# More row tokens, packed remainders and remainders on GpSimd in a hybrid encoder block

## The reference, cut to what matters

```python
q = (xf @ w_pq).reshape(t, 8, 2, 128)
sc = jnp.einsum("thpd,hpnd->thpn", q, sub_keys)
vals, idx = lax.top_k(sc, 16)
...
best, pos = lax.top_k(cand, 16)
eidx = jnp.take_along_axis(cidx, pos, axis=-1)
g = jax.nn.softmax(best, axis=-1)
...
ue = jnp.take(u, it, axis=0)
act = gelu(jnp.einsum("td,tkd->tk", xt, ue)) * gt
ve = jnp.take(v, it, axis=0)
return jnp.einsum("tk,tkd->td", act, ve)
```

## Time and profile before

| | |
|---|---|
| runs (us) | 1620.82, 1621.73, 1619.15; median 1620.82 |
| profiled execution | span 1618.1 us; no separate time is recorded for it; the median of the runs is 2.7 us more |
| TensorE busy | 1570.4 us (97%) |
| VectorE busy | 1403.7 us (87%) |
| ScalarE, GpSimd busy | 641.8 us (40%), 624.0 us (39%) |
| DMA | 436.11 MB, mean 270 GB/s |
| granted TensorE clock | 9 tenths or more in 37 of 40 slices, 8 in three; 1.00 in the expert stage |

### The profile page before, as it was taken

One profiled execution on the slowest core, in us unless ns is written; L12 is line 12 of the kernel. 1 busy time (PEld: TensorE's weight loads), 2 busy tenths in 40 slices (PEclk: granted clock), 3 DMA queues, 4 the chain that ended last, 5 costly groups with the idle time before them and its releaser, 6 DMA issues.

```text
span 1618.1 us, 23763 instructions
## 1 busy us (share of the span) xinstructions
PE 1570.4 (97%) x7899; PEld 1291.7 (80%) x7899; DVE 1403.7 (87%) x2781; ACT 641.8 (40%) x955; POOL 624.0 (39%) x531
## 2 busy tenths in 40 slices
PE   6999999999999999999999999999999999999997
PEld 3777764665557899988888888898888888888886
DVE  6888877764999999979888998989999998989886
ACT  4234654241122666663333333333333333333233
POOL 0000000010555500016655666656555676767520
PEclk8999999989999999999999999999999999999998
DMA  8432215542212355589999999999999999999981
GB/s 349 167 150 79 79 52 197 221 155 78 92 72 73 106 205 199 209 307 402 402 380 386 375 380 389 394 392 387 355 396 358 387 362 398 347 380 355 403 301 64
DMA packets 127851, 436.11 MB, mean 270 GB/s; under 512 B 12832, under 2 KB 35360, under 8 KB 122016
## 3 DMA queue, kind: packets, MB, share of 16 engines
q1 hardware_dynamic: 74112, 247.92, 41.2%
q0 software_dynamic: 52224, 184.62, 29.6%
q10 hardware_dynamic: 1440, 2.62, 0.4%
HBM read 407.29 MB, written 27.79 MB: 269 GB/s over the span
## 4 chain that ended last, share of the span: by engine, by line
PE 71%; DVE 19%; DMA 4%; issue 3%; ACT 2%; POOL 0%; DVEq 0%; SPq 0%; ACTq 0%; POOLq 0%
PE ps L970 23%; PE ps L900 23%; PE ps L671 10%; PE ps L662 6%; PE ps L958 3%; DMA graw<-gmat 3%; PE ps L827 3%; DVE low L1886 2%; DVE Vs L1874 1%; DVE Us L1857 1%; DVE big L1886 1%; DVE att L1713 1%; DVE att L1724 1%; DVE big L1711 1%; DVE big L1729 1%
## 5 line engine op out<-in xcount | busy, mean ns | idle before, releaser
L970 PE MATMUL ps<-Vs,As 128*128 128x512 f32 x2286 | 535.6, 390 | 2.5 <-DVE As L1877 2.5
L970 PEld LDWEIGHTS ps<-Vs,As 128*128 128x128 f32 x2286 | 425.9, 188 | 86.1 <-DVE Vs L1874 1.6
L900 PE MATMUL ps<-xs,Us 128*128 128x336 f32 x2832 | 461.2, 318 | 5.1 <-DVE Us L1857 4.2
L900 PEld LDWEIGHTS ps<-xs,Us 128*128 128x128 f32 x2832 | 441.4, 188 | 22.6 <-issue 10.0
L594 POOL DMA_INDIRECT big<-pv,islot x176 | 255.9, 1454 | 144.6 <-DVE low L1916 50.9
L1338 ACT ACTIVATE big<-ps 128x352 f32<-128x352 f32 x96 | 44.7, 465 | 340.4 <-PE ps L900 281.2
L1874 DVE TENSOR_TENSOR Vs<-big,Vs 128x1024 fp32r<-128x1024 f32 x127 | 155.2, 1222 | 17.1 <-ACT Vs L1344 14.3
L662 PE MATMUL ps<-big 128*128 128x512 f32 (+1 forms) x416 | 160.3, 544 | 1.3 <-ACT big L1040 1.3
L1916 DVE SCALAR_TENSOR_TENSOR low<-big,low 128x1024 f32<-128x1024 f32 x128 | 157.0, 1280 | 0.0
L1344 ACT ACTIVATE Vs<-big 128x1024 fp32r<-128x1024 f32 x127 | 134.0, 1055 | 42.9 <-PE ps L970 40.7
L594 POOL DMA_INDIRECT low<-pu,islot x88 | 119.7, 1360 | 72.5 <-DVE colv L1886 53.9
(11 more groups left out here) (249 smaller groups left out, 2087.2 us busy)
## 6 DMA issues: line engine op xcount, KB each, us to landing
big<-puT SPq DMA_DIRECT2D x128, 512.0 KB, 3.5
big<-pv SPq DMA_DIRECT2D x64, 1024.0 KB
big<-stream SPq DMA_DIRECT2D x31, 1024.0 KB, 5.2
gmat<-big SPq DMA_DIRECT2D x11, 2048.0 KB, 7.3
graw<-gmat SPq DMA_DIRECT2D x30, 512.0 KB
low<-wada SPq DMA_DIRECT2D x28, 512.0 KB, 4.8
work<-wada SPq DMA_DIRECT2D x14, 512.0 KB, 5.6
graw<-gmat SPq DMA_DIRECT2D x15, 384.0 KB
```

The source lines that it names most:

```text
L900: mm = nc.tensor.matmul(ps[:, 6 + e, DEAD:ET], a, xs[:, b, k, :], start=(k == 0 and a is hi and b == 0), stop=(k == KT - 1 and a is lo))
L970: mm = nc.tensor.matmul(ps[:, 2 * b + half, :], a, v_parts[:, w, half * T:(half + 1) * T], start=(opens and a is hi and w == 0), stop=(las ...
```

## The change

- The row tokens grow from 176 to 192: 64 of block 1 instead of 48 (NEXT = 4, XTOK = 64). NROWS becomes 192, XB 64, ET 320; 80 turns of the gate matrix are built, in ten pieces. The dots lie in groups 2 to 61, the additions in 62 to 123.
- `As` holds, for each slot, 640 columns: 64 of remainders, the 320 rounded values, 256 of remainders. For the first token block, whose 64 dense tokens fill half of a weight tile, the tile has remainders in one half of its columns and rounded values in the other. It is multiplied by V's rounded values and by V's remainders, 2 x 2 products instead of 3 x 2, and the two halves of the sum are added at the end by a product with a folding matrix. The other two blocks are as before.
- The activations' remainders are subtracted by GpSimd (`rest_a`), in two instructions of 64 and 256 columns, between its fetches. GpSimd's program is written out in full instead of looping; the index is read from `eidx`, without the copy to `islot`.
- V comes in another order from HBM, so that two tiles are one run of 8 KB on each partition.
- The fourth set of 16 extra tokens needs a fourth spread of normalised tokens (`repeat_ext`), a fourth accumulator and 16 more small DMAs. The fold moves from group 114 to group 126, into banks 6 and 7. The order of the last blocks is 0, 2, 1, 3.

The core of the diff:

```diff
-NEXT = 3
+NEXT = 4
...
-UB = 60
-VE = 122
+UB = 62
+VE = 124
...
-DEAD = XTOK - XB
+HALF = P - XB
+ORDER = (0, 2, 1, 3)
...
-        As = sb("As", [P, 2, 2, DT], f32r)
+        As = sb("As", [P, 2, 2 * ET], f32r)
...
+        def a_hi(A):
+
+            return A[:, HALF:HALF + ET]
...
+        def dots_by(o):
+
+            return NROWS * min(max(o - 1, 0), UB - 2) // (UB - 2)
+
+        def adds_by(o):
+
+            return NROWS * min(max(o - UB + 1, 0), VE - UB) // (VE - UB)
+
+        def taken_by(o):
+
+            return dots_by(o) + adds_by(o)
...
                 sp.wait_ge(vlo_ready, g * BODY + 2 * e + 2)
-                sp.dma_start(vraw[:, e % 2, :, :],
-                             pv[bass.ds((g * BODY + 2 * e) * P, 2 * P), :].rearrange("(a p) f -> p a f", p=P)
+                sp.dma_start(vraw[:, e % 2, :, :].rearrange("p a f -> p (a f)"),
+                             pvP[bass.ds(g * (BODY // 2) + e, 1), :, :].rearrange("a p f -> (a p) f")
                              ).then_inc(v_here[e % 2], 16)
...
-            def fetch(table, places, it, r0, first=False):
-                for half in range(2):
-                    if not first or half:
-                        pool.wait_ge(row_used, it * (2 * DOTS) + (r0 + half * DOTS - ROWBUF + 1))
-                    nc.gpsimd.tensor_copy(islot[:, half, :], eidx[:, bass.ds(it * (2 * DOTS) + half * DOTS, DOTS)]
-                                          ).then_inc(slot_copied, 1)
-                    pool.wait_ge(slot_copied, it * 2 + (r0 // DOTS + half + 1))
-                    nc.gpsimd.sem_inc(pool_turn, 1)
-                    for s in range(DOTS):
-                        r = half * DOTS + s
-                        if s and not (first and r < ROWBUF):
-                            pool.wait_ge(row_used, it * (2 * DOTS) + (r0 + r - ROWBUF + 1))
-                            nc.gpsimd.sem_inc(pool_turn, 1)
-                        nc.gpsimd.indirect_dma_start(
-                            out=places[r % ROWBUF], out_offset=None, in_=table,
-                            in_offset=bass.IndirectOffsetOnAxis(ap=islot[:, half, s:s + 1], axis=0)
-                            ).then_inc(row_here[r % ROWBUF], 16)
+            def fetch(r):
+
+                if r >= ROWBUF:
+                    pool.wait_ge(row_used, r - ROWBUF + 1)
+                if r == NROWS:
+                    pool.wait_ge(alo_ready, 2 * (EVERY * (-(-4 * D // ET)) + 3))
+                table, places, c = (pu, u_row, r) if r < NROWS else (pv, v_row, r - NROWS)
+                nc.gpsimd.indirect_dma_start(
+                    out=places[c % ROWBUF], out_offset=None, in_=table,
+                    in_offset=bass.IndirectOffsetOnAxis(ap=eidx[:, c:c + 1], axis=0)
+                    ).then_inc(row_here[r % ROWBUF], 16)
+
+            def rest_a(o):
+
+                A = As[:, o % 2, :] if o < XT - 1 else Al
+                if o % EVERY == EVERY - 1:
+                    act_t = early[:, o // EVERY, :]
+                else:
+                    act_t = gel[:, (o - o // EVERY) % 2, :]
+                hi = a_hi(A).bitcast(f32)
+                pool.wait_ge(ahi_ready, o + 1)
+                nc.gpsimd.tensor_tensor(A[:, 0:HALF], act_t[:, 0:HALF], hi[:, 0:HALF], ALU.subtract).then_inc(alo_ready, 1)
+                nc.gpsimd.tensor_tensor(A[:, HALF + ET:2 * ET], act_t[:, HALF:ET], hi[:, HALF:ET], ALU.subtract).then_inc(alo_ready, 1)
...
-            fetch(pu, u_row, 0, 0, True)
-            with pool.Fori(1, NROWS // (2 * DOTS)) as it:
-                fetch(pu, u_row, it, 0)
-            pool.wait_ge(alo_ready, EVERY * (-(-4 * D // DT)) + 3)
-            with pool.Fori(0, NROWS // (2 * DOTS)) as it:
-                fetch(pv, v_row, it, NROWS)
+            for r in range(ROWBUF):
+                fetch(r)
+            r = ROWBUF
+            for o in range(XT):
+                rest_a(o)
+                while r < 2 * NROWS and r - ROWBUF < taken_by(o):
+                    fetch(r)
+                    r += 1
...
-                        mm = nc.tensor.matmul(ps[:, 6 + e, DEAD:ET], a, xs[:, b, k, :],
+                        mm = nc.tensor.matmul(ps[:, 6 + e, 0:ET], a, xs[:, b, k, :],
...
             def output_block(o, b, a_parts, v_parts, last=False, opens=False):
-                hi, lo = (a_parts[:, w, b * P:(b + 1) * P] for w in range(2))
-                for a, w in ((hi, 0), (hi, 1), (lo, 0)):
+                if b == 0:
+                    both = a_parts[:, 0:P]
+                    pairs = ((both, 0), (both, 1))
+                else:
+                    hi, lo = (a_parts[:, c + b * P:c + (b + 1) * P] for c in (0, ET - HALF))
+                    pairs = ((hi, 0), (hi, 1), (lo, 0))
+                for i, (a, w) in enumerate(pairs):
                     for half in range(2):
                         mm = nc.tensor.matmul(ps[:, 2 * b + half, :], a, v_parts[:, w, half * T:(half + 1) * T],
-                                              start=(opens and a is hi and w == 0), stop=(last and a is lo))
+                                              start=(opens and i == 0), stop=(last and i == len(pairs) - 1))
                 return mm
 
+            def fold_halves(src, part, begins=False, ends=False):
+
+                for half in range(2):
+                    mm = nc.tensor.matmul(ps[:, 6 + half, :], part, src[:, half * T:(half + 1) * T],
+                                          start=begins, stop=ends)
+                return mm
...
             def last_two():
...
                     output_block(o + 1, b, Al, Vl, True).then_inc(v_done, 1)
+                    if b == 1:
+                        pe.wait_ge(unfolded_ready, 1)
+                        fold_halves(unfolded, fold, ends=True).then_inc(folded, 1)
...
-                    if last and d == 2:
+                    if last and d == BODY - 2:
+                        pe.wait_ge(gel_ready, XT + 2)
                         pe.wait_ge(row_used, NROWS + XTOK)
                         for q in range(NEXT):
-                            for half in range(2):
-                                nc.tensor.matmul(ps[:, half, :], gath[q], acc_ext[q][:, half * T:(half + 1) * T],
-                                                 start=False, stop=False)
+                            fold_halves(acc_ext[q], gath[q], begins=(q == 0))
...
-            f(piece[:, FIRST % PRING, :, 0:DEAD], zeros[:, 0:DEAD].unsqueeze(1).broadcast_to([P, NK, DEAD]), ACT.Copy)
...
-                dve.wait_ge(ahi_ready, o + 1)
-                v.tensor_tensor(A[:, 1, XB:DT], act_t, A[:, 0, XB:DT].bitcast(f32), ALU.subtract).then_inc(alo_ready, 1)
...
+        "pvP": A(peer_v)[0].reshape(XT // 2, 2, P, D).transpose(0, 2, 1, 3).reshape(XT // 2, P, 2 * D),
```

More of the change, by code:

```diff
@@ L86, with build @@
 BANKS = 4
-def build(nc, stream, wada, skT, xT, cols, rows, biasd, identd, puT, pu, pv, gmat, hsave, out):
+def build(nc, stream, wada, skT, xT, cols, rows, biasd, identd, puT, pvP, pu, pv, gmat, hsave, out):
     f32, f32r, i32, u32 = mybir.dt.float32, mybir.dt.float32r, mybir.dt.int32, mybir.dt.uint32
@@ L358, in build, with pslot, all_stored @@
         y_sum, y_sq, y_std, y_out = sem("y_sum"), sem("y_sq"), sem("y_std"), sem("y_out")
+        def pslot(k):
+            return (k - FIRST) % PRING
         def stored(k):
-            return 16 * sum(1 for q in range(FIRST, k) if q % PRING == k % PRING)
+            return 16 * sum(1 for q in range(FIRST, k) if pslot(q) == pslot(k))
+        def all_stored(eng):
+            for k in range(PIECES, PIECES + PRING):
+                eng.wait_ge(piece_out[pslot(k)], stored(k))
         def rest_after(n):
             return (n - GAP) * BUILT // (EARLY + 1 - GAP) + 1
+        def dots_by(o):
[4 more added lines that the diff above has]
+            return dots_by(o) + adds_by(o)
         def freed(eng, n):
@@ L502, in load_turn @@
                     if first and e == 2:
-                        for k in range(PRING):
-                            sp.wait_ge(piece_out[k], stored(PIECES + k))
+                        all_stored(sp)
                     if not (first and e < 2):
@@ L1249, in _, with repeat_ext @@
                 f(n_tok[:, half * T:(half + 1) * T], ps[:, 6 + half, :], ACT.Copy).then_inc(side_free, 1)
-            for q in range(NEXT):
+            def repeat_ext(q):
                 f(nrep[q].rearrange("p k (h t) -> p k h t", h=PH),
@@ L1254, in _ @@
                   ).then_inc(spread_ready, 1)
+            for q in range(NEXT - 1):
+                repeat_ext(q)
             def gelu_early(n):
@@ L1336, in dense_turn @@
                         before = 3 if d % EVERY < 2 else 2
[L1337 removed]
+                        act.wait_ge(alo_ready, o * 2 + 2 * (1 + 3 - before))
                         f(gel[:, i % 2, :], ps[:, 6 + i % 2, 0:ET], ACT.Gelu).then_inc(gel_ready, 1)
@@ L1362, in _ @@
             dense_turn(TURNS - 1, True)
-            for b in range(TB):
-                deviation(b)
```

(31 more changed lines are left out.)

115 lines of the change are left out of this document (57 added, 58 removed).

## The result

The changed kernel takes 1683.49 us, median of 4 runs (1679.81 to 1686.2), against 1620.16 us before (4 runs beside it): ratio 1.0387, 95% interval 1.0369 to 1.0405. Its profiled span is 1677.6 us, 59.5 us more than before. The forecast was 1669 us with a range of 1604 to 1716: direction and size came out, the mechanism only in part.

The account below looks back on a forecast made before the run. TensorE bounds the kernel before; after, VectorE plus GpSimd's subtractions at 7.32 (dots) and 7.45 us a group (additions) against 6.95: +53, less 5 outside, +48 on 1620.8 gives 1669 us, range 1604 to 1716.

Parts of the forecast that it names:

- TensorE's bound lifted: Expert stage: TensorE sets the pace before; fewer output products and narrower hidden products take it from 6.84 to 6.28 us a group.
- VectorE by itself, 6.05 and 6.18: Expert stage: VectorE's own work after the change, 6.05 us a group in the dots and 6.18 in the additions.
- The port, 1.02 us added to VectorE: Expert stage: GpSimd's two subtractions and VectorE take turns, adding 1.02 us a group: 7.07 in dots, 7.20 in additions.
- The rival in which the port costs part of its length: Expert stage: a held instruction's fixed part runs meanwhile, 6.9 to 7.05 us a group, total 1610 to 1628; chance 0.11.
- Both engines near 7.2, VectorE sets the end: Expert stage: GpSimd's queue, 6.2 to 8.0 us a group, middle 7.1, is as near the bound as VectorE, 7.07 and 7.20.
- The rival with 8.0: Expert stage: GpSimd's queue is the bound at 8.0 us a group, +123 us, total 1744; chance 0.09.
- The added 0.25: Expert stage: loss of two engines taking turns at the same load, 0.25 us a group, giving 7.32 in dots, 7.45 in additions.
- The start: Before the expert stage: 80 instead of 84 turns of the gate matrix, with less work in them, save 6.5 us.
- The transfers, 6.83 and 6.70 us at 404 GB/s: Expert stage: DMA needs 6.83 us a group in dots and 6.70 in additions, hidden under 7.3 and the next limit.
- The rival of the free port: Expert stage: GpSimd and VectorE don't hold each other up, DMA is the bound, 1593 to 1605 us; chance 0.15.
- The end, +3.7: Kernel end: 8 instead of 6 folding products, +1.9 us; second output block waits for 20 products instead of 12, +1.8.
- What would show it: Expert stage signs: subtractions much over 0.29 and 0.72 us, VectorE near 99%, TensorE 90% or less awaiting As, DMA 0.92.

Follow-up runs that it names:

- the best version: Changed kernel with both subtractions back on VectorE and rows spread over groups 2 to 125 instead of 2 to 123: 1603.75 us, ratio to before 0.9915.
- two such runs: Changed kernel without every fourth row fetch: 1630.34 us; changed kernel without every fourth dot and addition on VectorE: 1646.27 us.

## Why the prediction was right, and where it was wrong

From 1618.1 to 1677.6 us the span grew by 59.5: 8.5 up to the first output product, 50.0 from there to the last two groups (which start at 1597.8 before and 1656.3 after), 1.0 in the end.

- **TensorE's bound lifted: right.** Before, its own stream set the pace; with the subtractions on VectorE the groups run at 6.90 and 6.68 us with 34 matmuls.
- **VectorE by itself, 6.05 and 6.18: right.** It is 6.14 and 6.20 in the run without remainders.
- **The port, 1.02 us added to VectorE: this term is mis-sized.** In the changed kernel VectorE is busy 259.47/39.0 = 6.65 and 287.82/42.5 = 6.77 us a group: 0.51 and 0.57 more than its need, half of the term. "I take the upper one" was the wrong end. The rival in which the port costs part of its length, given 0.11, had this price right, but its 1610 to 1628 us had nothing for GpSimd's queue. The whole-instruction rule of the Trainium skill (SBUF — State Buffer, Who interferes with whom) gave 1.02 too: that there is a conflict agrees, its price on VectorE doesn't. The other side of it is on GpSimd: 2.03 us for 1.02 of work.
- **"Both engines near 7.2, VectorE sets the end": this step failed in the dots.** GpSimd's queue was put between 6.2 and 8.0, and the middle, 7.1, was taken. By the two windows it is 3.2 x 1.52 for the fetches + 1.98 for the subtractions + 0.90 idle = 7.7 in the dots, and 3.1 x 1.33 + 2.10 + 0.88 = 7.1 in the additions. The hope that the gap of 0.30 between fetches would shrink without the loop is not borne out: it stayed. The rival with 8.0 named the right mechanism for the dots and was given 0.09; its 2.7 for a group's subtractions was too much, and in the additions a fetch takes 1.33. There the groups run at 7.05, with GpSimd's queue full and VectorE at 96%, and the runs don't tell which sets the end.
- **The added 0.25: right for the wrong reason.** Over the 6.95 us of the prediction, 60 x 0.74 + 62 x 0.10 = 51 us stands against a forecast of 22 + 31 = 53. The sum fits, the halves don't: the dots lost twice what was forecast, the additions a fifth.
- **The start: missed.** -6.5 for the shorter building came (6.1). That the first remainder stands behind the store of the gate matrix and eight fetches (715.34 to 725.34 us) was not seen; it cost 14.7 us, of which the 6.1 gave back a part: the 8.5 us above. The prediction had asked what is queued behind the remainders, not what they are queued behind.
- **The transfers, 6.83 and 6.70 us at 404 GB/s: right**, as measured with the subtractions taken away: 6.84 and 6.71, at 403 and 408. They were not the bound here. The 435 GB/s that the prediction takes from the Trainium skill (DMA: Bandwidth & Descriptors, Where 436 GB/s comes from) are a ceiling of the SBUF side; for transfers between HBM and SBUF the same section has the HBM side bind at about 358. Neither is what these runs show: 398 to 408 GB/s, held over 300 us.
- **The rival of the free port** was to decide below 0.6 us of VectorE's time. VectorE lost less than that, and the kernel was slower all the same. Its price was 1593 to 1605 us; the best version, in which GpSimd only fetches, reaches 1603.75.
- **The end, +3.7:** 1.0 of it is in the last two groups; the two more folding products were not told apart.
- **What would show it:** the subtractions grew long, VectorE's operations beside them too, TensorE waits for As and is at 85 and 92%, and the DMA share fell to 0.94 in the dots. VectorE near 99% didn't come (86% in the dots), and that was the sign that should have told the two mechanisms apart.

## What to carry to other kernels

Before work goes to an idle engine, write down that engine's queue in full: each instruction at the length it has beside the others, the gap before each, and what stands ahead of the first one; GpSimd was busy 39% of the span, but 61 to 63% of the stage that counts, and two subtractions a group filled its queue. A small two-input operation on GpSimd costs twice beside a stream of two-input VectorE operations: it waits for the running one to end, and it holds the next. When two engines come out near the same load in a prediction, the terms of both have to be worked out to the same care, and a run that takes work off only one of them is the way to tell which it is. Here two such runs told it for the dots, and not for the additions.

## What was not expected of the hardware

- GpSimd pays more than VectorE: of the 1.72 us of a subtraction of 256 columns beside additions, 1.0 is waiting and 0.72 its own, and VectorE loses 0.51 to 0.57 us a group for 1.02 us of GpSimd's work.
- A copy with one input waits as long as a subtraction with two (0.40 us alone, 1.41 beside additions) but costs VectorE only 0.18 us over three additions. Memsets of 32 and 48 columns take 138 and 152 ns and cost it nothing that shows: dots and additions stand at 1221 and 1282 ns, against 1280 for the additions before.
- Whether it is the second input or the shorter time of its own that spares VectorE was not tried.
- The granted clock between 100 and 300 us was 1.00 in some profiled executions and 0.98 in others, and the expert stage then starts 5 us later; kernels with the same code up to there show both. Differences of that size between two totals are not read as an effect of an edit.
